# Compressed attention branch: block tiles with positions as the stationary operand, keys and values side by side, built by GpSimd; one merge gate block divided around the branch

## The reference, cut to what matters

```python
def compress_blocks(kv, pe, w1, w2):
    ...
    sub = kv.reshape(b, g, n_sub, CMP_STRIDE, d)
    blocks = jnp.concatenate([sub[:, :, r:r + n_cmp] for r in range(ratio)], axis=3)
    blocks = (blocks + pe).reshape(b, g, n_cmp, CMP_LEN * d)
    return jax.nn.silu(blocks @ w1) @ w2
```

## Time and profile before

| | us |
|---|---|
| Median of 3 runs | 1477.94 (1477.8 to 1478.58) |
| The profiled execution, its own time | 1478.09 |
| Its span, first to last instruction | 1476.3 |
| TensorE busy in the span | 1436.4 (97%) |
| VectorE, ScalarE, GpSimd busy | 780.8, 536.6, 152.0 |

### The profile page before, as it was taken

The page is one execution under the profiler, slowest core; times in us unless marked ns, Lnnn a source line. Parts: engine busy times, 40 slices in busy tenths (PEclk is TensorE's granted clock), DMA queues, the critical chain, the costliest instruction groups (busy, mean ns, idle before and its releaser), DMA issues.

```text
span 1476.3 us, 17308 instructions
## 1 busy us (share of the span) xinstructions
PE 1436.4 (97%) x7234; PEld 1167.2 (79%) x7234; DVE 780.8 (53%) x1029; ACT 536.6 (36%) x752; POOL 152.0 (10%) x125
## 2 busy tenths in 40 slices
PE   7999999899999999989999999999999999999997
PEld 6888688688888888868877687777878888888886
DVE  6998573644233343375683744564445455435533
ACT  5222433543332232254543316662343232212214
POOL 1030023100000000210240202110220000000002
PEclk9999999999999999989999979999999999999999
DMA  7323125013223232323324001102322323233222
GB/s 202 103 86 115 57 86 170 30 58 113 88 88 113 86 107 93 100 86 93 86 66 137 29 29 58 44 16 60 112 91 81 113 86 107 93 91 109 86 86 58
DMA packets 137966, 129.56 MB, mean 88 GB/s; under 512 B 14640, under 2 KB 134464, under 8 KB 137888
## 3 DMA queue, kind: packets, MB, share of 16 engines
q1 hardware_dynamic: 136752, 124.78, 27.2%
q0 software_dynamic: 992, 3.47, 0.8%
q10 hardware_dynamic: 144, 0.20, 0.0%
HBM read 126.34 MB, written 2.10 MB: 87 GB/s over the span
## 4 chain that ended last, share of the span: by engine, by line
PE 95%; ACT 1%; DVE 1%; DMA 1%; POOL 0%; issue 0%; SPq 0%; ACTq 0%
PE gemm L446 76%; PE gemm L847 3%; PE gemm L554 3%; PE misc L874 2%; PE misc L892 1%; PE gemm L593 1%; PE misc L704 1%; PE gemm L649 1%; PE misc L793 1%; DMA w_raw<-in_w_in 1%; PE misc L863 1%; PE gemm L863 1%; PE gemm L604 1%; POOL w_lo L2054 0%; PE misc L502 0%
## 5 line engine op out<-in xcount | busy, mean ns | idle before, releaser
L1452 DVE TENSOR_TENSOR w_lo<-w_raw,w_hi 128x2048 fp32r<-128x2048 f32 (+1 forms) x108 | 245.3, 2271 | 189.2 <-ACT w_hi L979 189.1
L446 PE MATMUL gemm<-h_hi,w_hi 128*128 128x512 f32 x864 | 341.3, 395 | 0.0
L446 PE MATMUL gemm<-h_hi,w_lo 128*128 128x512 f32 x864 | 337.8, 391 | 0.0
L446 PE MATMUL gemm<-h_lo,w_hi 128*128 128x512 f32 x864 | 337.8, 391 | 0.0
L979 ACT ACTIVATE w_hi<-w_raw 128x2048 fp32r<-128x2048 f32 (+1 forms) x113 | 213.8, 1892 | 143.9 <-PE gemm L446 139.5
L446 PEld LDWEIGHTS gemm<-h_hi,w_hi 128*128 128x128 f32 x864 | 163.3, 189 | 37.2 <-issue 2.7
L446 PEld LDWEIGHTS gemm<-h_lo,w_hi 128*128 128x128 f32 x864 | 163.2, 189 | 34.3 <-issue 1.0
L446 PEld LDWEIGHTS gemm<-h_hi,w_lo 128*128 128x128 f32 x864 | 163.1, 189 | 34.3
L446 PE MATMUL gemm<-n_hi,w_hi 128*128 128x512 f32 x352 | 137.4, 390 | 1.6 <-DVE n_lo L1964 1.6
L446 PE MATMUL gemm<-n_lo,w_hi 128*128 128x512 f32 x352 | 137.0, 389 | 0.0
L446 PE MATMUL gemm<-n_hi,w_lo 128*128 128x512 f32 x352 | 137.0, 389 | 0.0
(11 more groups left out here) (402 smaller groups left out, 1789.9 us busy)
## 6 DMA issues: line engine op xcount, KB each, us to landing
w_raw<-in_w_in SPq DMA_DIRECT2D x62, 512.0 KB, 4.6
w_raw<-in_w_down SPq DMA_DIRECT2D x32, 512.0 KB, 4.1
w_raw<-in_w_up SPq DMA_DIRECT2D x28, 512.0 KB, 4.6
w_raw<-in_w_ffn_gate SPq DMA_DIRECT2D x22, 512.0 KB, 4.5
w_raw<-in_w_ffn_up SPq DMA_DIRECT2D x22, 512.0 KB, 4.5
w_raw<-in_w_ffn_down SPq DMA_DIRECT2D x16, 512.0 KB, 4.2
w_raw<-in_w_o SPq DMA_DIRECT2D x8, 512.0 KB, 4.0
w_raw<-in_w_out SPq DMA_DIRECT2D x8, 512.0 KB, 4.1
```

The source lines that it names most:

```text
L446: mm = nc.tensor.matmul(bank[:], w(s)[:, kt, col0:col0 + P], x(n), start=first, stop=last)
L1452: V.tensor_tensor(part(lo_of(s), s), part(raw_of(s), s), f(part(hi_of(s), s)), SUB).then_inc(S("lo_done"), 1)
```

## The change

**The hidden layer.** A new tile `ZP` (also named `cmp_windows`) holds, for keys and values (2), for 16 tile indices j, and for two groups of 32 columns, the windows with their positions added. The tile is 128 x 64 for each kv and j, and is now the *stationary* operand; `W1` (128 x 128) moves. Keys write partitions 0 to 63 of one PSUM bank, values 64 to 127, alternating. So `hidden` comes out with windows on partitions and hidden units along the row, and the position column, the bias and its two instructions go.

**The silu and a transpose.** One tanh by ACT straight from PSUM and one DVE product, for keys and values together, then one transpose by TensorE and a copy by ACT to `cmp_hidden_T`, from which the second layer reads.

**GpSimd** builds `ZP` from `RAWC` in 16 additions of 64 partitions x 8 x 31, each waiting for the one before, ahead of its cosine products. In each the inner step of the read is 16 floats. `PES` is a copy of the positions with the two halves of the partitions exchanged. The copies by DVE and ACT go.

**The order.** On TensorE the hidden layer moves ahead of gate block 5; gate block 6 is cut in three parts, of 8, 4 and 12 matmuls. On DVE `ob_lo` moves behind `v_cmp_blocks`, since `ZP` lies where `ob_lo` is written. The tile `RS4` is moved by 1 KB.

```diff
+    ZP = at("cmp_windows", [2, 16, 2 * 32], f32, R1 + 48)
+    HT, HX = at("cmp_tanh", [P], f32, R1 + 64.5), at("cmp_hidden", [P], f32, R1 + 65)
...
+        pe.wait_ge(S("cmp_loaded"), 16 * 4)
+        pe.wait_ge(S("gpsimd_step"), WINDOWS_DONE)
+        bank = take(2)
+        for j in range(16):
+            for kv in range(2):
+                mm = nc.tensor.matmul(bank[64 * kv:64 * kv + 64, 0:P], ZP[:, kv, j, :], W1[kv][:, j, :], start=j == 0, stop=j == 15)
+        mm.then_inc(S("hidden_full"), 1)
         gate_block(5)
-        for kv in range(2):
-            bank = take(2 + kv)
-            for j in range(16):
-                mm = nc.tensor.matmul(bank[:, 0:66].rearrange("p (g n) -> p g n", n=33), W1[kv][:, j, :],
-                                      Z[:, 2 * kv:2 * kv + 2, 2 * j:2 * j + T + 1:16], start=j == 0, stop=j == 15)
-            mm.then_inc(S("hidden_full"), 1)
-        gate_block(6)
-        pe.wait_ge(S("hidden_ready"), 1)
+        def gate_part(x, first, last):
+            s = s0 + 12 + x // 2
+            m, b = BLOCKS_BEFORE[s] + x % 2, x % 2
+            if first == 0:
+                pe.wait_ge(S("lo_done"), s + 1)
+                pe.wait_ge(evac[m % 4], m // 4 + 1)
...
+        misc[2].wait(pe)
+        nc.tensor.transpose(take(3)[:, 0:P], HX[:], IDENT[:]).then_inc(S("hidden_T"), 1)
+        gate_part(6, 0, 8)
+        misc[3].wait(pe)
...
+        gate_part(6, 8, 12)
...
+        gate_part(6, 12, 24)
         gate_block(7)
...
+        mk = BLOCKS_BEFORE[PH["small"][0] + 7]
+        for kv in range(2):
+            pool.wait_ge(*evac_at(mk + kv))
+            for g in range(2):
+                rows = slice(64 * g, 64 * g + 64)
+                sub = RAWC[rows, kv, :].rearrange("p (n j h) -> p h j n", j=8, h=2)
+                for h in range(2):
+                    pe_cols = (PE_COLS if g == h else PES)[rows, kv, :]
+                    for jj in range(2):
+                        gstep.wait(pool)
+                        gstep.inc(Q.tensor_tensor(ZP[64 * h:64 * h + 64, kv, 8 * jj:8 * jj + 8, 32 * g:32 * g + N_CMP],
+                                              sub[:, h, :, jj:jj + N_CMP],
+                                              pe_cols[:, 8 * jj:8 * jj + 8].unsqueeze(2).broadcast_to([64, 8, N_CMP]), ADD))
```

More of the change, by code:

```diff
@@ L276, in build @@
     RESET = at("chunk_start", [T], f32, R1 + 59)
-    RS4 = at("gla_roots", [T], f32, R1 + 55)
+    RS4 = at("gla_roots", [T], f32, R1 + 56)
     SQH = [SQ[0][:], SQ[1][:], KL[:, 0, :], KL[:, 1, :]]
@@ L796, in _ @@
-        gate_block(6)
-        pe.wait_ge(S("hidden_ready"), 1)
+        pe.wait_ge(S("cmp_loaded"), 16 * 4)
[5 more added lines that the diff above has]
+        mm.then_inc(S("hidden_full"), 1)
+        gate_block(5)
+        def gate_part(x, first, last):
[4 more added lines that the diff above has]
+                pe.wait_ge(evac[m % 4], m // 4 + 1)
+            for n in range(first, last):
+                w, y = ((hi_of, HHI), (hi_of, HLO), (lo_of, HHI))[n % 3]
+                mm = nc.tensor.matmul(G[m % 4][:], w(s)[:, n // 3, P * b:P * b + P], y[:, n // 3, :], start=n == 0, stop=n == 23)
+            if last == 24:
+                mm.then_inc(S("block_full"), 1)
@@ L798, in _ @@
+        misc[2].wait(pe)
+        nc.tensor.transpose(take(3)[:, 0:P], HX[:], IDENT[:]).then_inc(S("hidden_T"), 1)
+        gate_part(6, 0, 8)
+        misc[3].wait(pe)
         bank = take(0)
         for g in range(2):
-            mm = nc.tensor.matmul(bank[64 * g:64 * g + 64, 0:N_CMP], W2[0][:], HX[0][:, 32 * g:32 * g + N_CMP], start=True, stop=True)
+            mm = nc.tensor.matmul(bank[64 * g:64 * g + 64, 0:N_CMP], W2[0][:], HXT[:, g, 0:N_CMP], start=True, stop=True)
         mm.then_inc(S("kc_full"), 1)
-        pe.wait_ge(S("hidden_ready"), 2)
@@ L803, in _ @@
         bank = take(1)
         for g in range(2):
-            mm = nc.tensor.matmul(bank[0:32, 64 * g:64 * g + 64], HX[1][:, 32 * g:32 * g + 32], W2[1][:], start=True, stop=True)
+            mm = nc.tensor.matmul(bank[0:32, 64 * g:64 * g + 64], HXT[:, 2 + g, :], W2[1][:], start=True, stop=True)
         mm.then_inc(S("vc_full"), 1)
+        gate_part(6, 8, 12)
         misc[0].wait(pe)
@@ L1295, in _ @@
             gate_out(x)
-        for n in range(4):
-            kv, g = n // 2, n % 2
-            A_(Z[64:128, n, 0:T - 1], RAWC[64 * g:64 * g + 64, kv, 1:T], ACT.Copy).then_inc(S("windows_b"), 1)
         split(15)
+        act.wait_ge(S("hidden_full"), 1)
+        A_(HT[:], M[2][:, 0:P], ACT.Tanh, scale=0.5).then_inc(S("hidden_tanh"), 1)
+        act.wait_ge(S("hidden_T"), 1)
+        A_(HXT[:].rearrange("p k n -> p (k n)"), M[3][:, 0:P], ACT.Copy).then_inc(read[3], 1)
         act.wait_ge(S("ob_lo_ready"), 4)
-        for kv in range(2):
-            act.wait_ge(read[2 + kv], 15)
-            A_(HT[kv][:], HX[kv][:], ACT.Tanh, scale=0.5).then_inc(S("hidden_tanh"), 1)
         gate_out(4)
@@ L1885, in _ @@
         ins.then_inc(read[1], 1)
+        for hd in range(GLA_H):
+            dve.wait_ge(S("ob_hi_ready"), hd + 1)
+            V.scalar_tensor_tensor(OBLO[:, hd, :], OSB[:, hd, :], 0.5, f(OBHI[:, hd, :]), MUL, SUB).then_inc(S("ob_lo_ready"), 1)
         for g in range(2):
```

47 lines of the change are left out of this document (13 added, 34 removed).

## The result

The changed kernel takes 1461.89 us (median, 1459.08 to 1463.39 in 4 executions) where the kernel before, run beside it, takes 1478.14 (1477.8 to 1478.58): ratio 0.989, 95% interval 0.9875 to 0.9904. It is faster by 16.3 us, 1.1%.

The account below looks back on a forecast made before the run. TensorE was taken to bound the kernel. Terms -2.5 - 8.0 - 1.8 + 0.4 = -11.9 and -1.6 took the 1476.3 us span to 1462.8; plus 1.8 outside it, 1464.6, less 0.15 to the median: 1464.5, range 1462.2 to 1469.0.

Parts of the forecast that it names:

- the wait: TensorE's idle time ahead of the hidden layer goes if GpSimd's additions are in time: -2.5 us.
- the hidden layer: Its 64 instructions at 0.061 us each, as in L745, take 3.9 us in place of 11.94: -8.0 us.
- gate block 6: Behind the hidden layer, at full clock, it takes 5.66 us in place of 7.43: -1.8 us.
- added: transpose, gate block 5: On TensorE's path, 0.2 us for the transpose and 0.2 for another return to gate matmuls: +0.4 us, bounds 0.2 and 0.8.
- the soft term: Half clock at the scores and gate block 7 may vanish (3.3 us gained) or stay (0); the middle taken, -1.6 us.
- the place where the cover ends: Ahead of the hidden layer, TensorE waits only if GpSimd's additions end after 838.1, about 4 us before the layer.
- The second rival: GpSimd's late additions slow DVE's two-input products, such as `gla_gate`, without stopping the layer: 1467 us, chance 0.15.
- What hides the rest: TensorE's matmuls cover silu, copies, `ob_lo` and the softmax over windows: price 0, though about 0.1 us comes through at the scores.
- A spell at the new layer: First rival: half clock returns at the new hidden layer, costing 3.3 us: 1468 us, chance 0.12 shared with serial halves.
- serial halves: First rival's other form: the hidden layer's halves run one behind the other, 7.2 us not 3.9: 1468 us, shared chance 0.12.
- The gain given back: Rival: a step behind gate block 7 waits for something unmoved, up to half the gain lost: 1471 us, chance 0.05.
- Slower than before through GpSimd: Rival: additions at over 2.65 us each make TensorE wait ahead of the layer beyond all gains: 1480.2 us, chance 0.04.

Follow-up runs that it names:

- before_no_wait: Kernel before with DVE's `ob_lo` moved behind `v_cmp_blocks`, and the waits for it by ACT and GpSimd moved; 1468.88 us, ratio 0.9943.
- weights_stationary: Changed kernel with `W1` stationary again in the hidden layer, order and additions kept; transpose and copy left unread; 1467.19 us, ratio 0.9931.
- additions_twice: Changed kernel with each of GpSimd's 16 additions made twice, 32 in all; 1465.61 us, ratio 0.9924.
- additions_34: Changed kernel with 34 GpSimd additions in place of 16, layer's new form kept; 1468.41 us, ratio 0.9951.
- additions_40: Changed kernel with 40 GpSimd additions in place of 16; 1472.68 us, ratio 0.9974.
- none_between: Changed kernel with gate block 6 halved, 12 matmuls before and 12 after small products and scores together; 1462.41 us, ratio 0.9905.
- undivided: Changed kernel with gate block 6 whole ahead of the small products; run twice, 1463.94 us (0.9911) and 1463.2 us (0.9915).
- sparse_34: Changed kernel with both 34 GpSimd additions and `W1` stationary again; 1477.16 us, ratio 0.9998.

## Why the prediction was right, and where it failed

In the section, by the prediction's own steps, with the kernel after as profiled:

| step | forecast | measured | from |
|---|---|---|---|
| the wait | -2.5 | -2.5 | 2.51 to none |
| the hidden layer | -8.0 | -8.3 | 11.94 to 3.65 |
| gate block 6 | -1.8 | -1.5 | 7.43 to 1.85 + 1.14 + 2.95 |
| scores and gate block 7 | -1.6 | -3.4 | 4.96 + 7.56 to 3.69 + 5.44 |
| added: transpose, gate block 5 | +0.4 | +0.3 | 0.11; 5.49 to 5.67 |
| the mask | 0 | -0.1 | 0.56 to 0.45 |
| sum | -13.5 | -15.5 | 41.04 to 25.53 |

**The step that failed** is the soft term, "-1.6, the middle" of 0 to 3.3 for the half clock at the scores. In the profile all of it was gained (3.4), as in two of three profiles of the kernel after. The third has a short spell, which stretches scores and last part from 3.69 + 2.95 to 3.87 + 4.33, 1.6 us, so that 1.8 of 3.4 are gained there. So the mechanism was right and the size off: one number stood for cases that the execution decides. The middle fits the short spell, and the ten profiles with gate block 6 in parts show none in four, the short one in five and one of 6.8 us. The term accounts for 1.8 of the 2.0 us that the section gained beyond the forecast.

**The range failed** for a second reason, the spread of executions, and here luck has its part. The medians of the kernel after were 1461.9, 1461.4 and 1462.9, so the third lies inside the range, and the gains in the three groups were 16.3, 16.3 and 13.0 us, where 13.5 were forecast. The low end was the profiled execution of before less the largest gain (1476.3 - 11.9 - 3.3 + 1.8 = 1462.9, or about 1462.6 with the 0.15 to the median and the added terms at their lower bound; the rest down to 1462.2 has no term of its own), as if an execution of before or after had one time. The first runs of before lay at 1477.8 to 1478.6, in the upper part of the 1474.0 to 1479.5 that 41 others show, and the kernel after alone spreads over 5 us, through half-clock spells in untouched code. As a ratio the forecast was 1464.5 / 1477.94 = 0.9909; the three groups gave 0.989, 0.9894 and 0.9908, and the first interval ends at 0.9904. Allowing 2 us for that spread, the low end would have been near 1460.

**The hidden layer** was right in size, and by the row taken for it: L745 at 0.061 each forecast 3.9, and 3.65 / 64 = 0.057 were measured, weight loads included. The rule of the Trainium skill, "TensorE: Matmul & The Clock Gate", Part 3 (Packing small matmuls), by which the loads would not have overlapped and the layer taken an estimated 7.3 us, does not hold in this trace. But the prediction put all 8.0 on the layer's form. By `before_no_wait` and `weights_stationary` about half of it is clock, and no profile lost that clock at the layer without idle time ahead. The reason given for gate block 6, no idle time and the denser form, names two changes; in the profiles each was enough alone (no idle time with the sparse form: 5.46; waits of 3.5 us with the dense one: layer 3.71, gate block 5 5.67). Over the section the clock is 4.4 (layer) + 2.0 (gate block 6, 7.43 to 5.46) + 1.3 (scores) + 2.1 (gate block 7) = 9.8 us, the form 3.9, the wait 2.5, and what was added takes back 0.7.

**GpSimd** was right in its result: 16 additions in 13.0 us, 0.81 each with the handoff, where 0.95 were forecast, and 10.2 us in hand. The Trainium skill's 50% for steps over 8 bytes ("GPSIMD Engine Reference", section 7) cannot be seen: a 248-element addition with a step of 64 bytes takes 0.73, no longer than the contiguous 256-element subtraction at 0.846. It takes a fifth more than the 0.61 that its share of a 512-element product would be. Wrong was the place where the cover ends. From the last addition to the layer it takes 5.8 to 5.9 us in `additions_twice`, `additions_34` and `additions_40`, not 4, since the rotary sums take 1.76 and 1.25 beside the cosine products; so the cover ends nearly 2 us earlier than at 838.1. The second rival's mechanism is real, past the slack that the kernel leaves, but smaller: the `gla_gate` products took up to 1.27 in place of 0.69 (1.74 assumed), and TensorE lost 0.6 there. One thing no rival had: an addition that starts with a split takes 2.79.

**What hides the rest** held step for step: the silu with 3.2 us in hand (forecast 3.7), `ob_lo` in 2.50 (2.8) and ended before the scores, the softmax over windows 1.4 ahead of its readers (1.4). Nothing was given back behind gate block 7: the two profiles are 19.0 us apart there and at the end.

**The rivals.** A spell at the new layer came in none of the three profiles, and serial halves neither. The gain given back: no. Slower than before through GpSimd: `additions_40`, with 24 additions more, is still 0.26% faster than before.

**Open** remain what decides whether the spell behind the scores comes (0, 0 and 3.4 us in the kernel after, 0 in `none_between`, 6.8 twice in `undivided`, 3.4 or 6.8 in five of the six others with gate block 6 in parts), and so how much of the gain the division of gate block 6 carries; and where the seven late executions of `sparse_34` lost their time.

## What to carry to other kernels

Price a short idle time of TensorE with what comes behind it: here one DVE step in the way cost 2.5 us of waiting, and with the sparse matmuls behind it some 5 us more (in the medians) at half clock, and moving that step alone gave half of the whole gain. Where the small operand can be the stationary one and the outputs can alternate between the halves of the partitions, 64 matmuls cost 3.65 us instead of 7.1 to 7.5. And give a forecast built on one profile the spread of the kernel's own executions on top of its unknown costs, and write out the cases of a soft term, each with its time, where the execution decides between them.

## What the runs showed of the hardware

- At the hidden layer half clock came where idle time and sparse matmuls met, not always, and with neither of them alone in the profiles taken unless the idle time was long (7.5 us). Elsewhere it came without idle time ahead: behind the scores, in eight of twelve profiles of the new order. Sparse without idle time: 1.00 in both profiles (7.09 and 7.55 us). Dense behind three waits of 3.5 us in sum: 1.00. Sparse behind 2.5 us of idleness, in the kernel before: 13.7 us at 0.50, and the layer took 11.94. Sparse behind 3.5 us: 1.00 in the one profile taken, and 7 of 10 executions some 9 us longer than that one.
- Matmuls of 64 stationary columns that alternate between the halves of the partitions written issue every 0.057 us with 128 f32 columns moving; 128 stationary columns with 64 moving every 0.111 (7.09 / 64).
- In code that no run changed there are spells near 275 and 635 us in all fourteen profiles, for 6.8 to 10.3 us, and near 16, 180 and 664 us in some of them, for 3.4 us, which makes executions of one kernel differ by some 5 us.
- GpSimd and DVE slow each other where both have two inputs. Beside DVE's products GpSimd's additions take 1.07 to 1.08 us in place of 0.73, and DVE's products 1.27 in place of 0.69; an addition that started with DVE's split of 128 x 2048 took 2.79, and the split its usual 2.23.
